# Three weight slots split in place, GLU products and folds on VectorE, convolution taps that alternate between chunks, gate units first, loops written out

## The chip, the cores and the metric

The kernel runs on one core of one Trainium2 chip. Its time is the device time of one launch in microseconds (us). A core has a matrix engine (TensorE, PE in the profile), a vector engine (VectorE, DVE), an activation engine (ScalarE, ACT), a general one (GpSimd, POOL), and a queue that issues transfers (SyncE, SP). Each works through its own program in order; they meet at semaphores only.

## The reference, cut to what matters

Two transformer blocks run over 1024 positions of width 1024, the second also over 256 context positions in its first layer, all in fp32.

```
h = x + swa(rms(x));  h = h + relu(rms(h) @ w_up)**2 @ w_down;  x = rms(h)     # first block
# second block, even layer (for x and for ctx)
a_val, a_glu, a_gate, b_val, b_gate = split(pre(x) @ w_in)                      # five times 512
u   = a_val * sigmoid(a_glu)
u   = silu(layernorm(dwconv31(u) + conv_b))
y_a = (u @ pw + pw_b) * silu(a_gate)
y_b = fourier(b_val) @ fw * silu(b_gate)        # DFT over positions and over groups of 128 channels
x   = x + gate * (concat(y_a, y_b) @ w_out)
# odd layer: cb*dwconv3(cc*cx)*silu(cg) beside RoPE window attention with context keys, then w_out
# out = rms(x)
```

## The kernel before, in words

Activations lie with channels on the 128 partitions and positions along the free axis, in tiles of 512 (TILES1: two tiles; TILES2: these and one of 256 for the context). Every fp32 matmul is made of three (mm3, L188): both operands are cut into a high half of type fp32r and a low half, the rest; high times high, high times low and low times high are summed in PSUM.

The weights are 153 units of 128 x 1024 fp32 (512 KB) in the order in which they are used, counted by stages: qkv 10, wo 8, mlp 64, ein 20 (the even layer's input projection, from E0), dft 6, fw 1, pw 2, eout 8, oin 26 (from O0), oout 8. A unit is loaded by SP (load_unit, L135) into one of two slots wst, its high half is cast by ScalarE (split_hi, L152), and its low half is subtracted by GpSimd (split_lo, L158), into slots wH and wL. In a few places GpSimd makes both halves (split_unit, L141). The copy into a slot waits until TensorE has begun the unit after the one that used it (units_begun), and the load until the low half made from the raw slot is done (weights_split). linear_unit (L194) then runs 48 matmuls for two tiles, or 72 for three, and ScalarE or VectorE drains the banks. The units of a stage are a hardware loop (Fori) over pairs, on each engine.

The program is a sequence of blocks, each ended by a barrier of all engines. The first unit of a stage is split in the block before, the second after the barrier, beside the norm, whose diagonal scalings (norm_sq, L398) and squares (L250, L255) run on VectorE and ScalarE.

In the block of the even input projection (from L1174) the units come as four pairs a_glu, a_val, then four of b_val, then eight gate units. ScalarE drains them into sig and val, bt, or a gate buffer that is stored to memory. GpSimd multiplies sig and val into conv_in; VectorE then runs the 31 taps of the depthwise convolution of chunk c, one after the other (L1294 the first, L1298 the rest; each waits for the one before), 4 x 31 in all, each 128x1295. GpSimd also folds each b_val unit into sums and differences (bf) for the Fourier part, and makes its low half bL after ScalarE's copies to bH:

```
                        pool.tensor_tensor(bf[:, 0:512], bt[:, 0:512], bt[:, 512:1024], ALU.subtract).then_inc(fold_step, 1)
                        pool.wait_ge(fold_step, 2 * g + 1)
                        pool.tensor_tensor(bt[:, 0:512], bt[:, 0:512], bt[:, 512:1024], ALU.add).then_inc(fold_step, 1)
```

The next block (from L1353) has on TensorE: sums of the convolved tiles for the layer norm (L1364), the channel DFT, the DFT over positions with four dft units and three halves out of two more, then the mixing with fw and pw. VectorE meanwhile scales by the reciprocal root (L1506, L1510), and ScalarE applies silu (L1478) and copies high halves (L1480, L1487). In this block GpSimd splits all units alone (stream of split_unit).

Of the kernel before, what the change touches and what calls it, by code (L numbers as in the profile page):

```python
# [24 lines left out]
ALU = mybir.AluOpType  # L25
# [5 lines left out]
P = 128  # L31
# [3 lines left out]
CTX = 256  # L35
# [50 lines left out]
def build(nc, t):  # L86
# [13 lines left out]
    with es:  # L100
# [32 lines left out]
        W_FREE = 2  # L133

        def load_unit(sp, base, i, s):  # L135
            u, slot = base + 2 * i + s, (base + s) % 2
            sp.wait_ge(weights_split, u + 1)
            sp.dma_start(wst[:, slot, :], t["wstream"][bass.ds(u, 1)].rearrange("a p f -> p (a f)"))\
                .then_inc(stage_loaded[slot], 16)

        def split_unit(pool, base, i, s):  # L141
            u, slot = base + 2 * i + s, (base + s) % 2
            pool.wait_ge(stage_loaded[slot], ((base + s) // 2 + 1 + i) * 16)
            pool.wait_ge(units_begun, u + 1)

            pool.tensor_tensor(wH[:, slot, :], wst[:, slot, :], ones[:, 0:1].to_broadcast([P, KC * P]), ALU.mult)\
                .then_inc(weights_hi, 1)
            pool.wait_ge(weights_hi, u + 1)
            pool.tensor_tensor(wL[:, slot, :], wst[:, slot, :], wH[:, slot, :].bitcast(F32), ALU.subtract)\
                .then_inc(weights_split, 1)  # L150

        def split_hi(act, base, i, s):  # L152
            u, slot = base + 2 * i + s, (base + s) % 2
            act.wait_ge(stage_loaded[slot], ((base + s) // 2 + 1 + i) * 16)
            act.wait_ge(units_begun, u + 1)
            act.copy(wH[:, slot, :], wst[:, slot, :]).then_inc(weights_hi, 1)  # L156

        def split_lo(pool, base, i, s):  # L158
            u, slot = base + 2 * i + s, (base + s) % 2
            pool.wait_ge(weights_hi, u + 1)  # L160
            pool.tensor_tensor(wL[:, slot, :], wst[:, slot, :], wH[:, slot, :].bitcast(F32), ALU.subtract)\  # L161
                .then_inc(weights_split, 1)

        def stream(eng, one, lo, hi):

            if (hi - lo) // 2 > 1:
# [1885 lines left out]
```

## Time and profile before

| | |
|---|---|
| timed runs | 2345.18, 2348.38, 2345.18 us; median 2345.18 |
| profiled execution | 2351.11 us, its span 2349.1 us |
| TensorE busy | 2171.5 us (92%), 10132 matmuls; granted clock 0.95 in the mean |
| VectorE busy | 1264.1 us (54%) |
| ScalarE busy | 728.0 us (31%) |
| GpSimd busy | 700.5 us (30%) |
| moved by DMA | 157.16 MB, 67 GB/s in the mean |

Busy times are sums over the span. An engine's share says how full it is, not whether the end of a block waits for it. A row of the timeline is: start, duration, engine, line, operation, output <- inputs, count, and in brackets how long the engine stood before it and what released it.

### The profile page before, as it was taken

The numbers are of one execution on the slowest core, as the hardware profiler recorded it, in microseconds if no ns is written. First come the engines' busy times: TensorE is split into PE (matmuls) and PEld (weight loads), VectorE is DVE, ScalarE is ACT, GpSimd is POOL, SyncE is SP. The second block draws the span as 40 slices with busy tenths as digits, with TensorE's granted clock in tenths as the row PEclk, the third lists the DMA queues.
The fourth block names the chain that finished last, engine by engine and source line by source line (L and its number), as shares of the span: only waits on it lengthen the run. The fifth ranks groups of instructions, "written<-read, shape, count | busy, mean of one in ns | idle before, by whom it ended". The sixth has DMA issues, their size and how long they took to land. (4 is left out here: it accounts for less than half of the span.)

```text
span 2349.1 us, 29236 instructions
## 1 busy us (share of the span) xinstructions
PE 2171.5 (92%) x10132; PEld 1766.1 (75%) x10132; DVE 1264.1 (54%) x1972; ACT 728.0 (31%) x1358; POOL 700.5 (30%) x359
## 2 busy tenths in 40 slices
PE   4999989999999999999889889979989999979896
PEld 3876668788888888888578778668867788766675
DVE  6137852672371371473669999785252122378724
ACT  4236542421221220222442122432152211156522
POOL 4223322322222222222244762142132222234422
PEclk9987889899999999999899989989999999979998
DMA  4100021231231231231201012124121211100031
GB/s 137 67 27 1 1 89 46 81 127 52 72 134 45 76 129 45 89 116 49 113 27 36 29 66 82 56 75 177 36 111 45 81 45 53 45 5 14 10 116 72
DMA packets 42690, 157.16 MB, mean 67 GB/s; under 512 B 4224, under 2 KB 8960, under 8 KB 41344
## 3 DMA queue, kind: packets, MB, share of 16 engines
q1 hardware_dynamic: 40176, 146.49, 17.9%
q10 hardware_dynamic: 2448, 9.84, 1.1%
q8 instruction: 36, 0.59, 0.1%
q14 instruction: 30, 0.25, 0.0%
HBM read 136.39 MB, written 19.92 MB: 67 GB/s over the span
## 5 line engine op out<-in xcount | busy, mean ns | idle before, releaser
L161 POOL TENSOR_TENSOR wL<-wst,wH 128x1024 fp32r<-128x1024 f32 x139 | 360.3, 2592 | 1139.8 <-ACT wH L156 1139.5
L190 PE MATMUL banks<-u2H,wH 128*128 128x512 f32 x736 | 295.7, 402 | 29.4 <-POOL wL L161 18.6
L191 PE MATMUL banks<-u2L,wH 128*128 128x512 f32 x736 | 291.5, 396 | 0.0
L192 PE MATMUL banks<-u2H,wL 128*128 128x512 f32 x736 | 291.1, 396 | 0.0
L190 PE MATMUL banks<-uH,wH 128*128 128x512 f32 x672 | 262.7, 391 | 2.0 <-DVE uL L387 1.5
L191 PE MATMUL banks<-uL,wH 128*128 128x512 f32 x672 | 262.2, 390 | 0.0
L192 PE MATMUL banks<-uH,wL 128*128 128x512 f32 x672 | 262.2, 390 | 0.0
L1298 DVE SCALAR_TENSOR_TENSOR conv_out<-conv_in,par,conv_out x120 | 242.1, 2018 | 21.6 <-DVE conv_out L1298 20.9
L190 PE MATMUL banks<-aH,wH 128*128 128x512 f32 x640 | 249.9, 390 | 2.2 <-PEq L213 2.2
L191 PE MATMUL banks<-aL,wH 128*128 128x512 f32 x640 | 249.5, 390 | 0.0
L192 PE MATMUL banks<-aH,wL 128*128 128x512 f32 x640 | 249.5, 390 | 0.0
L156 ACT CAST wH<-wst 128x1024 fp32r<-128x1024 f32 x139 | 145.3, 1045 | 332.7 <-PE banks L190 326.7
L190 PEld LDWEIGHTS banks<-u2H,wH 128*128 128x128 f32 x736 | 141.4, 192 | 66.3 <-issue 32.3
L1072 DVE TENSOR_TENSOR h<-banks,h 128x512 f32 x64 | 43.9, 690 | 232.3 <-PE banks L192 232.3
L191 PEld LDWEIGHTS banks<-u2L,wH 128*128 128x128 f32 x736 | 141.4, 192 | 29.6 <-issue 1.2
L192 PEld LDWEIGHTS banks<-u2H,wL 128*128 128x128 f32 x736 | 141.0, 192 | 30.2
L1060 DVE SCALAR_TENSOR_TENSOR mod_junk<-mod_w,cvec 128x1024 bf16<-128x1024 f32 x96 | 146.8, 1529 | 14.3 <-DMA mod_w<-in_mod_w 2.8
L190 PEld LDWEIGHTS banks<-uH,wH 128*128 128x128 f32 x672 | 126.6, 188 | 31.5 <-issue 5.1
L192 PEld LDWEIGHTS banks<-uH,wL 128*128 128x128 f32 x672 | 126.6, 188 | 26.6
L191 PEld LDWEIGHTS banks<-uL,wH 128*128 128x128 f32 x672 | 126.7, 189 | 26.2
L190 PEld LDWEIGHTS banks<-aH,wH 128*128 128x128 f32 x640 | 120.5, 188 | 27.6 <-PEq L213 2.6
L191 PEld LDWEIGHTS banks<-aL,wH 128*128 128x128 f32 x640 | 120.5, 188 | 25.1
(279 smaller groups left out, 4012.0 us busy)
## 6 DMA issues: line engine op xcount, KB each, us to landing
wst<-in_wstream SPq DMA_DIRECT2D x153, 512.0 KB, 3.3
mod_w<-in_mod_w SPq DMA_DIRECT2D x48, 512.0 KB, 6.0
x_scratch<-h SPq DMA_DIRECT2D x2, 4096.0 KB, 11.8
gt<-gates_scratch SPq DMA_DIRECT2D x8, 640.0 KB, 4.0
h<-in_x SPq DMA_DIRECT2D x4, 1024.0 KB, 10.7
h<-in_x SPq DMA_DIRECT2D x1, 4096.0 KB, 12.1
h<-x_scratch SPq DMA_DIRECT2D x1, 4096.0 KB, 12.2
xo<-x_scratch SPq DMA_DIRECT2D x1, 4096.0 KB, 12.2
```

The source lines that it names most:

```text
L156: act.copy(wH[:, slot, :], wst[:, slot, :]).then_inc(weights_hi, 1)
L161: pool.tensor_tensor(wL[:, slot, :], wst[:, slot, :], wH[:, slot, :].bitcast(F32), ALU.subtract)\
L190: first = pe.matmul(out, aH, bH, start=start, stop=False)
L191: pe.matmul(out, aH, bL, start=False, stop=False)
L192: return first, pe.matmul(out, aL, bH, start=False, stop=stop)
L1060: dve.scalar_tensor_tensor(mod_junk[:], mod_w[:, m, :], 1.0, cvec[:, v, :], ALU.mult, ALU.mult, accum_out=modv[:, bass.ds(12 * q + 3 * i + ...
L1072: dve.tensor_tensor(dst, bank(4 + s * 2 + ti), dst, ALU.add).then_inc(down_drained, 1)
L1298: dve.scalar_tensor_tensor(dst, src, w, dst, ALU.mult, ALU.add).then_inc(conv_step, 1)
```

## The change

There are three slots, raw, whose low half is written over the raw weights (wL is the same memory), and wH beside them. A load waits for units_begun of the unit two before, and a cast waits for its load alone. ScalarE makes all high halves and GpSimd all low ones (lows). Two units of the next stage are split before a barrier. The loops are written out. In the even projection VectorE makes the products, the folds and the low halves of b; taps alternate over the chunks whose input is there, seven per unit; the gate units come before those of b_val.

```diff
-        wst = sb("wst", [2, KC * P], A_WST)
-        wH = sb("wH", [2, KC * P], A_WHL, F32R)
-        wL = sb("wL", [2, KC * P], A_WHL + 8 * KB, F32R)
-
-
-        stage_loaded = [sem("stage_loaded0"), sem("stage_loaded1")]
+        R = 3
+        raw = sb("raw", [R, KC * P], A_WST)
+        wL = sb("wL", [R, KC * P], A_WST, F32R)
+        wH = sb("wH", [R, KC * P], A_WST + R * 4 * KB, F32R)
...
+        def load_unit(sp, u):
+            if u >= R:
+                sp.wait_ge(units_begun, u - R + 2)
+            sp.dma_start(raw[:, u % R, :], t["wstream"][u]).then_inc(raw_loaded[u % R], 16)
 
         def loads(sp, first, last):
 
-            lo = W0[first] + 3 if W0[first] else 0
-            hi = min(W0[last] + dict(STAGES)[last] + 3, UNITS)
-            stream(sp, load_unit, lo, hi)
-
-        def splits(pool, first, last, done=1):
-
-            lo = W0[first] + done
-            hi = min(W0[last] + dict(STAGES)[last] + 1, UNITS)
-            stream(pool, split_lo, lo, hi)
+            lo = W0[first] + R - 1 if W0[first] else 2
+            for u in range(lo, min(W0[last] + dict(STAGES)[last] + R - 1, UNITS)):
+                load_unit(sp, u)
+
+        def split_hi(act, u):
+            if u < UNITS:
+                act.wait_ge(raw_loaded[u % R], (u // R + 1) * 16)
+                act.copy(wH[:, u % R, :], raw[:, u % R, :]).then_inc(weights_hi, 1)
+
+        def split_lo(eng, u):
+            if u < UNITS:
+                eng.wait_ge(weights_hi, u + 1)
+                eng.tensor_tensor(wL[:, u % R, :], raw[:, u % R, :], wH[:, u % R, :].bitcast(F32), ALU.subtract)\
+                    .then_inc(weights_split, 1)
+
+        def lows(pool, lo, hi):
+            for u in range(lo, hi):
+                split_lo(pool, u)
...
-            pe.wait_ge(weights_split, u + 1 + W_FREE)
+        def linear_unit(pe, u, j0, K, tiles, rhs, bank_of, done, drained, ready=None, off=0):
+
+            pe.wait_ge(weights_split, u + 1)
...
+                    if part == 1:
+                        load_unit(sp, 0)
+                        load_unit(sp, 1)
...
-                split_unit(pool, W0["qkv"], 0, 0)
-                split_unit(pool, W0["qkv"] + 1, 0, 0)
+                split_lo(pool, 0)
+                split_lo(pool, 1)
                 norm1.pool(pool)
-                splits(pool, "qkv", "qkv", 2)
+                lows(pool, 2, W0["wo"] + 2)
...
-                norm1.act(act)
+                norm1.act(act, lambda: (split_hi(act, 0), split_hi(act, 1)))
...
-                with act.Fori(0, 4) as i:
+                for i in range(0, 4):
                     for s in range(2):
                         hi(i, s, lambda ti: aH[:, bass.ds(2 * i + s, 1), TN * ti:TN * ti + TN].rearrange("p a n -> p (a n)"))
-                        split_hi(act, W0["qkv"] + 2, i, s)
+                        split_hi(act, 2 * i + s + 2)
                 hi(4, 0, lambda ti: kH[:, TN * ti:TN * ti + TN])
-                split_hi(act, W0["qkv"] + 10, 0, 0)
+                split_hi(act, 10)
                 hi(4, 1, lambda ti: vT[:, TN * ti:TN * ti + TN])
+                split_hi(act, 11)
...
+                for v in range(4):
+                    i, s = divmod(v, 2)
+                    act.wait_ge(b_lo, v + 1)
+                    for ti, (c0, n) in enumerate(TILES2):
+                        drain(i + 8, s, ti, bt[:, c0:c0 + n], ACT.Copy)
+                    split_hi(act, E0 + 18 + v)
+                    act.wait_ge(folded, v + 1)
+                    act.copy(bH[:, v, 0:SEQ], bf[:]).then_inc(b_hi, 1)
+                    act.copy(bH[:, v, SEQ:TOK], bt[:, SEQ:TOK]).then_inc(b_hi, 1)
...
-                pool.memset(conv_in[:], 0.0).then_inc(ci_zero, 1)
-                pool.wait_ge(ci_zero, 1)
-                with pool.Fori(0, HALF) as i:
-                    for s in range(2):
-                        split_lo(pool, E0 + 2, i, s)
-                    pool.wait_ge(ein_drained, (2 * i + 2) * T3 + E_FREE)
...
+                for at in (0, MAIN0 + SEQ, CTX0 + CTX):
+                    pool.memset(conv_in[:, :, at:at + PAD], 0.0).then_inc(consts_set, 1)
+                lows(pool, E0 + 2, W0["dft"] + 2)
...
+                def product(c):
+                    dve.wait_ge(ein_drained, (2 * c + 2) * T3 + E_FREE)
+                    dve.tensor_tensor(conv_in[:, c, MAIN0:MAIN0 + SEQ], sig[:, 0:SEQ], val[:, 0:SEQ], ALU.mult)
+                    dve.tensor_tensor(conv_in[:, c, CTX0:CTX0 + CTX], sig[:, SEQ:TOK], val[:, SEQ:TOK], ALU.mult)\
+                        .then_inc(ci_ready, 1)
+
+                def fold(g):
+                    dve.wait_ge(ein_drained, (g + 17) * T3 + E_FREE)
+                    dve.tensor_tensor(bf[:, 0:512], bt[:, 0:512], bt[:, 512:1024], ALU.subtract).then_inc(fold_step, 1)
+                    dve.wait_ge(fold_step, 2 * g + 1)
+                    dve.tensor_tensor(bt[:, 0:512], bt[:, 0:512], bt[:, 512:1024], ALU.add).then_inc(fold_step, 1)
+                    dve.wait_ge(fold_step, 2 * g + 2)
+                    dve.tensor_tensor(bf[:, 512:768], bt[:, 0:256], bt[:, 256:512], ALU.subtract)
+                    dve.tensor_tensor(bf[:, 768:1024], bt[:, 0:256], bt[:, 256:512], ALU.add).then_inc(folded, 1)
+
+                def fold_low(g):
+                    dve.wait_ge(b_hi, 2 * g + 2)
+                    dve.tensor_tensor(bL[:, g, 0:SEQ], bf[:], bH[:, g, 0:SEQ].bitcast(F32), ALU.subtract)
+                    dve.tensor_tensor(bL[:, g, SEQ:TOK], bt[:, SEQ:TOK], bH[:, g, SEQ:TOK].bitcast(F32), ALU.subtract)\
+                        .then_inc(b_lo, 1)
+
+                steps, tapped, latest = [0] * HALF, [0], [-1] * HALF
+
+                def taps(n, chunks):
+                    for _ in range(n):
+                        open_ = [c for c in range(chunks) if steps[c] < TAPS]
+                        if not open_:
+                            return
+                        c = min(open_, key=lambda c: latest[c])
+                        tap = steps[c]
+                        src = conv_in[:, c, tap:tap + CONV_OUT]
+                        dst = conv_out[:, c, :]
+                        w = par[:, PC["conv_w"] + c * TAPS + tap:PC["conv_w"] + c * TAPS + tap + 1]
                         if tap == 0:
-                            dve.tensor_scalar(dst, src, w, par[:, bass.ds(c + PC["conv_b"], 1)], ALU.mult, ALU.add)\
-                                .then_inc(conv_step, 1)
+                            dve.wait_ge(ci_ready, c + 2)
+                            dve.tensor_scalar(dst, src, w, pcol("conv_b", c), ALU.mult, ALU.add).then_inc(conv_step, 1)
                         else:
-                            dve.wait_ge(conv_step, c * TAPS + tap)
+                            dve.wait_ge(conv_step, latest[c] + 1)
                             dve.scalar_tensor_tensor(dst, src, w, dst, ALU.mult, ALU.add).then_inc(conv_step, 1)
+                        steps[c], latest[c] = tap + 1, tapped[0]
+                        tapped[0] += 1
+
+                for v in range(20):
+                    if v < 16:
+                        if v == 1:
+                            dve.wait_ge(consts_set, 4 + 3)
+                        if v < 8 and v % 2:
+                            product(v // 2)
+                        taps(7, min((v + 1) // 2, HALF))
+                    else:
+                        fold(v - 16)
+                        taps(4 if v < 18 else HALF * TAPS, HALF)
+                        fold_low(v - 16)
...
-                        loads(sp, "dft", "dft")
+                        for u in range(W0["dft"] + 2, W0["pw"] + 2):
+                            load_unit(sp, u)
+                    if i == 6:
+                        load_unit(sp, W0["eout"])
+                    if i == 7:
+                        load_unit(sp, W0["eout"] + 1)
...
-                stream(pool, split_unit, W0["dft"] + 1, W0["pw"] + 3)
+                lows(pool, W0["dft"] + 2, W0["eout"] + 2)
...
+                split_hi(act, W0["dft"] + 2)
...
+                    if j == 5:
+                        split_hi(act, W0["dft"] + 3)
+                split_hi(act, W0["dft"] + 4)
+                split_hi(act, W0["dft"] + 5)
...
+                    if j in (3, 7, 15):
+                        split_hi(act, W0["fw"] + (3, 7, 15).index(j))
...
-    units += [ein[12:16], ein[8:12], ein[16:20]]
+    units += [ein[8:12], ein[16:20], ein[12:16]]
```

The first place is ScalarE at the end of the block that projects q, k and v. Before, with kH and vT the last two units drained and the second branch the barrier:

```order
L156 CAST wH<-wst 128x1024 [waits units_begun]
L539 REGISTER_ALU
L539 COMPARE_AND_BRANCH
L538 CAST kH<-banks 128x512 [waits qkv_done] x2
L156 CAST wH<-wst 128x1024 [waits units_begun,stage_loaded0]
L538 COPY vT<-banks 128x512 [waits qkv_done] x2
L498 UNCONDITIONAL_BRANCH
L818 UNCONDITIONAL_BRANCH [waits barrier_Pool_Activation_PE_DVE_SP_release]
```

After:

```order
L149 CAST wH<-raw 128x1024 [waits raw_loaded0]
L515 CAST kH<-banks 128x512 [waits qkv_done] x2
L149 CAST wH<-raw 128x1024 [waits raw_loaded1]
L515 COPY vT<-banks 128x512 [waits qkv_done] x2
L149 CAST wH<-raw 128x1024 [waits raw_loaded2]
L473 UNCONDITIONAL_BRANCH
L795 UNCONDITIONAL_BRANCH [waits barrier_Pool_Activation_PE_DVE_SP_release]
```

One cast (raw_loaded2, unit 11, the second of the next stage) has moved in ahead of the barrier, behind the copy to vT, which was the last work of the block. The odd projection ends in the same way.

The second place is VectorE in the even projection. Before, the whole of it is this loop over a chunk's taps (the branch ahead of it enters it):

```order
L1287 UNCONDITIONAL_BRANCH
L1287 ISA
L1294 ISA [waits ci_ready]
L1294 ISA
L1294 REGISTER_ALU
L1294 TENSOR_SCALAR conv_out<-conv_in,par 128x1295
L1297 REGISTER_ALU
L1298 ISA [waits conv_step]
L1298 SCALAR_TENSOR_TENSOR conv_out<-conv_in,par,conv_out 128x1295
```

After, its last rows, for the last two units of b_val, which are units 18 and 19 of the stage:

```order
L1229 TENSOR_TENSOR bf<-bt 128x512 [waits ein_drained]
L1231 TENSOR_TENSOR bt<-bt 128x512 [waits fold_step]
L1233 TENSOR_TENSOR bf<-bt 128x256 [waits fold_step]
L1234 TENSOR_TENSOR bf<-bt 128x256
L1259 SCALAR_TENSOR_TENSOR conv_out<-conv_in,par,conv_out 128x1295 [waits conv_step] x11
L1238 TENSOR_TENSOR bL<-bf,bH 128x1024 [waits b_hi]
L1239 TENSOR_TENSOR bL<-bt,bH 128x256
L1238 TENSOR_TENSOR bL<-bf,bH 128x1024 [waits b_hi]
L1239 TENSOR_TENSOR bL<-bt,bH 128x256
L1140 UNCONDITIONAL_BRANCH
L1481 UNCONDITIONAL_BRANCH [waits barrier_Pool_Activation_PE_DVE_SP_release]
```

The last eleven taps now stand between the fold of unit 18 and its low halves, and the low halves of unit 19 are the last work before the barrier; its fold (four rows like the first four) stands between them.

The third place is ScalarE in the block of the Fourier part. Before, ahead of and among the silu jobs (zH is the channel DFT, ln_rs the root, sH the high half of a silu):

```order
L1467 CAST zH<-banks 128x512 [waits ln_z_done] x2
L1472 ACT_TABLE_LOAD
L1472 ACTIVATE ln_rs<-banks,eps 128x512 [waits ln_sq_used] x2
L1472 ACTIVATE ln_rs<-banks,eps 128x256 [waits ln_sq_used]
L1478 ACT_TABLE_LOAD
L1478 ACTIVATE conv_out<-conv_out,par 128x512 [waits ln_v]
L1480 CAST sH<-conv_out 128x512 [waits ln_silu]
```

After, up to the first silu job:

```order
L1447 CAST zH<-banks 128x512 [waits ln_z_done] x2
L149 CAST wH<-raw 128x1024 [waits raw_loaded2]
L1453 ACT_TABLE_LOAD
L1453 ACTIVATE ln_rs<-banks,eps 128x512 [waits ln_sq_used] x2
L1453 ACTIVATE ln_rs<-banks,eps 128x256 [waits ln_sq_used]
L1459 ACT_TABLE_LOAD
L1459 ACTIVATE conv_out<-conv_out,par 128x512 [waits ln_v]
L1461 CAST sH<-conv_out 128x512 [waits ln_silu]
```

and behind the last silu jobs:

```order
L1459 ACTIVATE conv_out<-conv_out,par 128x256 [waits ln_v]
L1461 CAST sH<-conv_out 128x256 [waits ln_silu]
L149 CAST wH<-raw 128x1024 [waits raw_loaded1]
L149 CAST wH<-raw 128x1024 [waits raw_loaded2]
L1472 ACTIVATE fH<-banks 128x512 [waits dft_done] x4
L149 CAST wH<-raw 128x1024 [waits raw_loaded0]
L1472 ACTIVATE fH<-banks 128x256 [waits dft_done]
```

Four casts of weights have come in, ahead of the root, behind the sixth job (not shown), and two between the last silu and the first fH; a fifth follows the fourth fH. They are work that GpSimd did.

## Rows read from the trace of the kernel before

**Rows 1.** A window of the MLP: us, busy times, PEclk, DMA share, GB/s.

```profile
840.00:900.00 60.00, 60.00 (x267) 49.67 (x266) 34.92 (x43) 12.33 (x17) 15.80 (x6) 1.00 0.30 105
```

**Rows 2.** The page: the span, TensorE's busy time, and one VectorE group.

```profile
span 2349.1 us, 29236 instructions
PE 2171.5 (92%) x10132; PEld 1766.1 (75%) x10132; DVE 1264.1 (54%) x1972; ACT 728.0 (31%) x1358; POOL 700.5 (30%) x359
L1072 DVE TENSOR_TENSOR h<-banks,h 128x512 f32 x64 | 43.9, 690 | 232.3 <-PE banks L192 232.3
```

**Rows 3.** The waits of TensorE: us in total, times, longest.

```profile
PE banks L190 <- POOL wL L161: 18.6, 4, 6.5
```

**Rows 4.** Windows of the even projection, and of its last five units.

```profile
1205.00:1475.60 270.60, 255.81 (x1297) 219.02 (x1296) 241.94 (x122) 58.03 (x87) 129.22 (x50) 0.96 0.15 53
1406.66:1475.60 68.94, 68.86 (x360) 59.19 (x358) 62.82 (x36) 14.52 (x22) 14.51 (x5) 1.00 0.23 86
```

**Rows 5.** The timeline of ScalarE behind unit 1 of the even projection.

```profile
1205.41 1.04 ACT L156 CAST wH<-wst 128x1024 fp32r<-128x1024 f32 x1
```

**Rows 6.** The timeline of VectorE where one chunk's taps end.

```profile
1418.08 1.57 DVE L1298 SCALAR_TENSOR_TENSOR conv_out<-conv_in,par,conv_out  x1 [0.18 <-DVE conv_out L1298]
1419.56 0.95 DVE L1294 TENSOR_SCALAR conv_out<-conv_in,par  x1
...
1424.19 3.44 DVE L1298 SCALAR_TENSOR_TENSOR conv_out<-conv_in,par,conv_out  x1 [0.18 <-DVE conv_out L1298]
```

**Rows 7.** The timeline of GpSimd in the even projection.

```profile
1408.89 2.40 POOL L161 TENSOR_TENSOR wL<-wst,wH 128x1024 fp32r<-128x1024 f32 x1 [13.55 <-ACT wH L156]
1422.59 3.67 POOL L161 TENSOR_TENSOR wL<-wst,wH 128x1024 fp32r<-128x1024 f32 x1 [11.30 <-ACT wH L156]
```

**Rows 8.** The timeline at the end of the even projection.

```profile
1479.08 1.57 DVE L1298 SCALAR_TENSOR_TENSOR conv_out<-conv_in,par,conv_out  x1 [0.18 <-DVE conv_out L1298]
...
1480.97 2.04 PE L1364 MATMUL banks<-conv_out,ones 128*128 128x512 f32 x2 [5.45 <-PEq L1174]
```

**Rows 9.** The timeline of the Fourier part and the mixing.

```profile
1514.58 1.90 POOL L146 TENSOR_TENSOR wH<-wst,ones 128x1024 fp32r<-128x1024 f32 x1 [47.54 <-PE banks L190]
...
1518.58 6.74 DVE L1510 SCALAR_TENSOR_TENSOR conv_out<-conv_out,par,ln_rs 128x512 f32<-128x512 f32 x4
...
1558.08 0.58 PE L190 MATMUL banks<-wH,zH 128*128 128x256 f32 x1 [10.46 <-DVE fL L1518]
...
1568.03 0.47 PE L190 MATMUL banks<-fH,wH 128*128 128x512 f32 x1 [1.96 <-DVE fL L1518]
...
1608.29 0.49 PE L190 MATMUL banks<-yH,wH 128*128 128x512 f32 x1 [2.26 <-PEq L213]
```

**Rows 10.** The timeline of VectorE at the start.

```profile
18.38 5.60 DVE L398 TENSOR_SCALAR norm_sq<-ident,rms_cols 128x128 f32<-128x128 f32 x4
23.90 8.20 DVE L255 TENSOR_TENSOR x_squares_acc<-x_squares_acc,x_squares_sq 128x512 f32<-128x512 f32 x8
```

**Rows 11.** The timeline at the end of the projection of q, k, v.

```profile
148.07 0.59 ACT L538 COPY vT<-banks 128x512 f32<-128x512 f32 x1 [4.85 <-PE banks L192]
...
148.96 0.29 PE L190 MATMUL banks<-kH,aH 64*128 64x128 f32 x1 [0.93 <-PEq L498]
```

**Rows 12.** The timeline of the norm ahead of the MLP.

```profile
422.21 3.23 PE L355 MATMUL banks<-inv_d,wo_squares_acc 128*128 128x1 f32 x16 [2.79 <-PEq L912]
...
424.28 3.01 DVE L398 TENSOR_SCALAR norm_sq<-ident,rms_cols 128x128 f32<-128x128 f32 x4
...
427.35 3.78 PE L360 MATMUL banks<-norm_sq,ones 128*128 128x512 f32 x4 [1.91 <-DVE norm_sq L398]
427.41 0.87 DVE L398 TENSOR_SCALAR norm_sq<-ident,rms_cols 128x128 f32<-128x128 f32 x4
```

**Rows 13.** The timeline at the end of the odd projection.

```profile
2042.90 0.62 ACT L1742 CAST ycH<-cw 128x512 fp32r<-128x512 f32 x1 [0.32 <-DVE cw L1820]
...
2044.87 0.59 PE L190 MATMUL banks<-k2H,qH 64*128 64x256 f32 x2 [3.44 <-PEq L1624]
```

More of the change, by code:

```diff
@@ L562, in lo @@
                             .then_inc(qkv_drained, 1)
-                with dve.Fori(0, 4) as i:
+                for i in range(0, 4):
                     for s in range(2):
@@ L943, in _ @@
                 dve.wait_ge(x_again, 16)
-                with dve.Fori(0, 4) as i:
+                for i in range(0, 4):
                     for s in range(2):
@@ L1001, in hidden @@
                 def hidden(q):
-                    with act.Fori(0, 4) as i:
+                    for i in range(0, 4):
                         for s in range(2):
@@ L1042, in hidden @@
                 def hidden(q):
-                    with dve.Fori(0, 4) as i:
+                    for i in range(0, 4):
                         for s in range(2):
@@ L1065, in down @@
                 def down(q, squares=None):
-                    with dve.Fori(0, 4) as i:
+                    for i in range(0, 4):
                         for s in range(2):
@@ L1106, in _ @@
                 down(0)
-                with pe.Fori(1, QUARTERS) as q:
+                for q in range(1, QUARTERS):
                     up(q, 0)
@@ L1286, in _ @@
                 norm4.dve(dve)
[L1287 to L1292 removed]
+                dve.sem_inc(ci_ready, 1)
+                dve.sem_inc(b_lo, 1)
@@ L1408, in _ @@
                     u = D0 + 4 + min(half, 1)
-                    slot = begin(u) if half < 2 else u % 2
+                    slot = begin(u) if half < 2 else u % R
                     if half == 0:
@@ L1580, in _ @@
                 dve.wait_ge(x_back, 32)
-                with dve.Fori(0, 4) as i:
+                for i in range(0, 4):
                     for s in range(2):
@@ L1715, in _ @@
                 act.sem_inc(S["ag_stored"], 16)
-                with act.Fori(0, 2) as i:
+                for i in range(0, 2):
                     for s in range(2):
@@ L1743, in branch @@
                             .then_inc(S["yc_hi"], 1)
-                    if not last:
-                        split_hi(act, O0 + 15, 2 * i, 0)
-                with act.Fori(0, 3) as i:
-                    branch(i, False)
-                branch(3, True)
+                    split_hi(act, O0 + 15 + 4 * i)
+                for i in range(4):
+                    branch(i)
             @block.vector
@@ L1780, in _ @@
                     rot_lo(0, ti, k2H[:, TN * ti:TN * ti + TN], k2L[:, TN * ti:TN * ti + TN])
-                with dve.Fori(0, 2) as i:
+                for i in range(0, 2):
                     for s in range(2):
@@ L1795, in _ @@
                 dve.wait_ge(S["prod_zero"], 2)
-                with dve.Fori(0, 4) as i:
+                for i in range(0, 4):
                     for ti in range(2):
@@ L1896, in _ @@
                 dve.wait_ge(x_back, 32 + 16)
-                with dve.Fori(0, 4) as i:
+                for i in range(0, 4):
                     for s in range(2):
```

264 lines of the change are left out of this document (82 added, 182 removed).

## The prediction

> **What bounds the kernel now.** I read the windows view first. In the linear stages TensorE is busy the whole 60.00 us of a window at a granted clock of 1.00, with 267 matmuls in it, about 0.225 us apart [rows 1]. There a weight unit of 48 matmuls takes 10.9 us. The page's span of 2349.1 us can only shrink where TensorE stands still, 177.6 us in all (2349.1 - 2171.5 us) [rows 2]. So I read TensorE's waits next. 18.6 us of them, in 4 waits with a longest of 6.5 us, are put down to GpSimd's low halves [rows 3]; the unit is cut late where GpSimd folds in between. Then come the windows of the even projection: from the end of unit 1 at 1205 to the end of unit 19 at 1475.6 TensorE idles 14.8 us (270.60 - 255.81) and the clock is 0.96; in the last five units it is 1.00 and a unit takes 13.8 us (68.94 / 5) [rows 4]. Eighteen units at 13.8 us are 248.2 us, so stalls and the low clock behind them cost 22.4 us. But that is not what the stage's end waits for: the last tap of the convolution ends at 1480.65, and only 0.3 us later, at 1480.97, TensorE starts the next block [rows 8]. VectorE is the second bound.
>
> **The change part by part**, in the time of the profiled execution.
>
> *Slots, loads, unrolling: 0 in the linear stages.* A unit must be loaded, cut (1.04 us of ScalarE [rows 5]) and subtracted within 10.9 us, before and after; the old order does it, since TensorE never waits there [rows 1], and the new one asks for the same work with a slot more. The window is full across loop ends too, so the gain of unrolling is 0 by it. The Trainium skill, page "Runtime: NRT & Kernel Launch", section "Instruction fetch mechanics", says that a taken branch can force a fetch stall; by that rule the sum would come out lower.
>
> *Even projection: -7.6.* TensorE loses its three stalls: unit n now ends at 1205.0 + 13.78 (n - 1), unit 16 at 1411.7, unit 18 at 1439.3, unit 19 at 1453.0. What then ends last is VectorE. A tap of the same chunk takes 1.57 us and waits 0.18 for the one before, together 1.75; behind another chunk it need not wait, and the one such row starts 1.48 us after its predecessor (1419.56 less 1418.08) [rows 6]. A tap that meets a GpSimd subtract takes 3.44 us for 1.57, and the subtract 3.67 us for 2.40 [rows 6, 7]: they take turns, and one low half per unit costs VectorE about 1.9 us. So seven alternated taps and one meeting are 12.3 us, under the 13.8 us of a unit; the first two units, with one open chunk, are 14.2 us, and the four products add 1.5 us each (an estimate: 1280 columns to a tap's 1295 [rows 6]). VectorE is through with unit 15's taps near 1401 and idles until unit 16 ends. Units 16 and 17: fold 2.5 + 2.4 (one meeting), four taps 6, low halves 1.5, together 12.4 us, in time. The tail begins at unit 18, 1439.7: fold 4.8, to 1444.5; eleven taps, four of them serial, 17.4; low halves 1.6, to 1463.5. Only now may ScalarE drain unit 19 (its buffer was in use): 1.4. Fold 4.8, the two copies 1.6, low halves 1.5, barrier 0.4: the next block starts at 1473.4, against 1480.97. Of the 22.4 us only 7.6 arrive, and TensorE stands about 20 us at the end instead. The Trainium skill, page "GPSIMD Engine Reference", section "Key points", says that GpSimd contends with VectorE instructions that have two SBUF inputs; the trace agrees, with 3.44 against 1.57 us. Bounds: without meetings in the tail -12.4; with all its taps serial (+1.9) and another meeting (+1.9) -3.8.
>
> *Transform and mixing, 1480.97 to 1608.29: -5.* Before, GpSimd made both halves (1.90 and some 2.4 us [rows 7, 9]) of six units while VectorE normalised, and four scalings took 6.74 us, which are 2.8 us at the 0.69 us that an operation of this size takes elsewhere [rows 2]. Now GpSimd makes four low halves there and the high halves sit in ScalarE's queue behind the silu jobs. I add up: the first cut delays ScalarE's root by 1.0; scalings and roots run undisturbed, so ScalarE is through six silu jobs at 1528.8 and cuts the fourth matrix, which is ready at 1532.3; TensorE wants it at 1530.2 and waits 2. All twelve jobs end at 1535.8, the fifth matrix is ready at 1539.3, TensorE waits 1.5, and its three halves of 5.8 us (48 matmuls of 256 columns, some 0.12 us each, an estimate) end at 1556.7 where before the last began at 1558.08, after the 10.46 us wait. The mixing starts near 1558.7 instead of 1568.03: -9.3. It gives back some: ScalarE waits for the unit of the pointwise weights, whose load can't start before the mixing does, so the first copies are 3 us late and TensorE ends 1.9 us later relative to its start. For two or three new short waits and the clock behind them I add 2.4, since each old stall in the projection cost 2.6 us of clock besides itself ((22.4 - 14.8) / 3) but shorter ones cost less. Bounds: -9 with no clock loss, +2 if the two waits and the late copies are double.
>
> *Start: -1.9.* Four diagonal scalings took 5.60 us beside GpSimd's two casts and two subtracts, and the second tile's squares ended at 32.1 [rows 10]. Now ScalarE casts before those squares (+2.1 on its side), the scalings take 0.87, as four of them do where GpSimd is idle [rows 12], and two subtracts remain: squares end near 30.2. Bounds -4 and +1 (weights now load before the second half of the input).
>
> *Ends of blocks: +8.0.* Every block ends in a barrier. Units n and n + 1 of the next stage are now cut before it, where the second was cut behind it. After the projection of q, k, v the last copy ends at 148.66 and TensorE starts at 148.96 [rows 11]; now 1.04 + 0.1 + 2.40 + 0.3 follow: 152.4, +3.4. Before the window attention likewise from 2043.52: 2047.4 for 2044.87, +2.5 [rows 13]. Before the MLP the barrier moves from 422.2 to 424.8, but there the 3.01 us of diagonals, in which GpSimd was in the way, become 0.87, so that the spread starts right after the 3.23 us of sums, at 428.0 for 427.35: +0.7 [rows 12]. The even and the odd projection begin with the same norm: +0.7 each. Bounds: 6 and 11.
>
> Sum: 0 - 7.6 - 5.0 - 1.9 + 8.0 = -6.5, hence 2344.6 us for the profiled execution's 2351.1. The three timed runs have a median of 2345.18, 5.9 us under it; taken off the median the sum gives **2338.7 us**.
>
> **Rivals.** (a) *The transform stage doesn't gain* (0 to +3 for -5): the matrices come late from ScalarE because its queue is in order. For it: eight cuts now stand between other jobs. Against it: VectorE is freed of some 15 us of meetings. About 2345, within 0.2%. (b) *Slower:* the alternated taps don't start earlier than 1.75 us. Then seven taps and a meeting are 14.2 us, more than a unit's 13.8, VectorE falls behind, the first fold starts near 1424, and the tail ends near 1489: +8 for -7.6, so 2354. It decides as soon as taps plus meeting exceed 13.8 us. Against it stands the one row of 1.48 us. (c) *More gain:* the tail has no meetings (-4.8) and the transform stage gives 9: 2330. (d) *Unrolled code starves an engine* and each linear unit gets a gap. The window of 267 matmuls would show it as idle time; 0.1 us for each of 139 units would be +14, 2352. Against it: the even transform's code is straight already, and its matmuls follow each other without gaps.
>
> **How the numbers follow.** Likeliest 2338.7, own range 2332 to 2345, chance 0.55; (a) 0.22; (b) 0.08; (c) 0.10; (d) 0.05. 0.2% is 4.7 us, about what a measurement of this kernel can tell from no change: faster is below 2340.5, slower above 2349.9. Of the likeliest case some 0.40 lies below 2340.5; with (c) and a little else faster is 0.52; slower 0.14; same 0.34. The range 2329 to 2349 leaves out (b), (d) and the far side of (c).
>
> **What would show it.** In the profile after: no wait on a GpSimd low half from 1205 to 1453 on TensorE; taps 1.48 us apart; a TensorE gap of about 20 us at the end of the even projection and a block start 7.6 us earlier relative to unit 1's end; the 10.46 us wait gone and two waits of 1 to 3 us on the new low halves before it; gaps of 4.4 and 6 us instead of 0.93 and 3.44 ahead of the two attentions; windows of 60.00 us busy in the MLP. Wrong would be: gaps inside linear units, or a tail that ends elsewhere than on VectorE.

## The result and the profile after

The changed kernel takes 2415.9 us in the median of four runs (2413.70 to 2417.95), where the kernel before took 2345.38 beside it: a ratio of 1.0293, 95% interval 1.0278 to 1.0308. It is 70.5 us slower. The forecast was 2338.7, with a range of 2329 to 2349. The profiled execution has a span of 2414.5 us, 65.4 more than before.

The page of the changed kernel: the span, the busy times, and the groups of the low halves and of the taps.

```profile
span 2414.5 us, 25481 instructions
PE 2162.0 (90%) x10132; PEld 1759.5 (73%) x10132; DVE 1215.8 (50%) x2004; ACT 733.1 (30%) x1366; POOL 687.1 (28%) x315
...
L154 POOL TENSOR_TENSOR wL<-raw,wH 128x1024 fp32r<-128x1024 f32 x153 | 490.5, 3207 | 1374.9 <-ACT wH L149 1374.9
...
L1259 DVE SCALAR_TENSOR_TENSOR conv_out<-conv_in,par,conv_out 128x1295 f32<-128x1295 f32 x120 | 181.4, 1579 | 0.6
```

TensorE has as many matmuls as before and is busy 9.5 us less [rows 2], so all of the loss is standing still: 252.5 us (2414.5 - 2162.0) where it was 177.6. Two rows say more than they seem to. A low half takes 3207 ns in the mean, though the same operation takes 2.40 us undisturbed [rows 7]: 153 times 0.8 is over 120 us of waiting inside the operation. (In the serial run below the mean is 2612 ns, so some 30 us of it are there without the stall too.) And the taps have 0.6 us of idle time ahead of them in all 120.

TensorE's waits after the change, answering to [rows 3]: us in total, times, longest.

```profile
PE banks L163 <- POOL wL L154: 81.3, 4, 71.5
...
PE banks L1342 <- PEq L1140: 18.2, 1, 18.2
PE banks L163 <- DVE win_pTL L739: 16.1, 20, 3.3
PE banks L163 <- DVE stat L728: 15.6, 4, 9.3
PE banks L163 <- PEq L185: 7.4, 3, 3.4
PE banks L163 <- PEq L1608: 5.8, 1, 5.8
```

One wait of 71.5 us is as large as the whole loss. The timeline of the changed kernel's GpSimd in the even projection shows where it comes from, and those of ScalarE, VectorE and TensorE around it what it is:

```profile
1242.31 11.50 POOL L154 TENSOR_TENSOR wL<-raw,wH 128x1024 fp32r<-128x1024 f32 x1 [11.26 <-ACT wH L149]
1256.09 2.50 POOL L154 TENSOR_TENSOR wL<-raw,wH 128x1024 fp32r<-128x1024 f32 x1 [2.28 <-ACT wH L149]
1269.87 11.47 POOL L154 TENSOR_TENSOR wL<-raw,wH 128x1024 fp32r<-128x1024 f32 x1 [11.28 <-ACT wH L149]
1283.65 2.50 POOL L154 TENSOR_TENSOR wL<-raw,wH 128x1024 fp32r<-128x1024 f32 x1 [2.31 <-ACT wH L149]
1297.95 83.31 POOL L154 TENSOR_TENSOR wL<-raw,wH 128x1024 fp32r<-128x1024 f32 x1 [11.81 <-ACT wH L149]
```

```profile
1310.59 1.04 ACT L149 CAST wH<-raw 128x1024 fp32r<-128x1024 f32 x1 [0.41 <-ACT val L1158]
```

```profile
1286.47 0.96 DVE L1256 TENSOR_SCALAR conv_out<-conv_in,par 128x1295 f32<-128x1295 f32 x1
1287.34 91.72 DVE L1259 SCALAR_TENSOR_TENSOR conv_out<-conv_in,par,conv_out 128x1295 f32<-128x1295 f32 x62
```

```profile
1381.31 0.80 PE L163 MATMUL banks<-u2H,wH 128*128 128x512 f32 x1 [71.55 <-POOL wL L154]
```

The subtract had its input at 1297.95 and nothing else to wait for, yet it ends at 1381.26. The 62 taps end at 1379.06 (1287.34 + 91.72), 2.2 us earlier, and 2.4 us is what a subtract takes by itself: of the 81 us before it got nothing done. The two of 11.5 us end in the same way, 2.3 us behind the end of a run of 14 taps. The next cast (1310.59) was in time, so the load and ScalarE are not it. Windows of the changed kernel: the one of the MLP, and then two behind the wait (columns as in [rows 1]).

```profile
840.00:900.00 60.00, 60.00 (x266) 49.70 (x265) 33.54 (x40) 12.47 (x17) 17.24 (x6) 1.00 0.23 79
```

```profile
1381.30:1386.30 5.00, 4.99 (x12) 3.92 (x13) 0.00 (x0) 0.00 (x0) 2.29 (x1) 0.51 0.40 108
1386.30:1521.70 135.40, 135.36 (x710) 116.62 (x708) 36.50 (x31) 27.21 (x42) 22.45 (x9) 1.00 0.22 65
```

Linear stages are full as before. Behind the wait the granted clock is 0.51 for 5 us, the lower of its two levels, which costs 2.5 more: 74.0 us in all, more than the 65.4 by which the span grew. The rest of the execution is 8.6 us shorter.

### The profile page after: what moved, and what is told of

Its sections match the earlier page's. It is cut to its first block and busy times, and to the rows that moved or that the text cites. A ratio compares the mean times of both kernels' runs of the same rounds, so it can differ in the third digit from the quotient of the medians.

```text
span 2414.5 us, 25481 instructions
## 1 busy us (share of the span) xinstructions
PE 2162.0 (90%) x10132; PEld 1759.5 (73%) x10132; DVE 1215.8 (50%) x2004; ACT 733.1 (30%) x1366; POOL 687.1 (28%) x315
## 5 line engine op out<-in xcount | busy, mean ns | idle before, releaser
L154 POOL TENSOR_TENSOR wL<-raw,wH 128x1024 fp32r<-128x1024 f32 x153 | 490.5, 3207 | 1374.9 <-ACT wH L149 1374.9
L149 ACT CAST wH<-raw 128x1024 fp32r<-128x1024 f32 x153 | 159.5, 1045 | 281.3 <-DMA raw<-in_wstream 276.5
L1259 DVE SCALAR_TENSOR_TENSOR conv_out<-conv_in,par,conv_out 128x1295 f32<-128x1295 f32 x120 | 181.4, 1579 | 0.6
L1039 DVE TENSOR_TENSOR h<-banks,h 128x512 f32<-128x512 f32 x64 | 43.9, 689 | 230.8 <-PE banks L165 230.8
L1027 DVE SCALAR_TENSOR_TENSOR mod_junk<-mod_w,cvec 128x1024 bf16<-128x1024 f32 x96 | 156.6, 1632 | 5.0
L165 PEld LDWEIGHTS banks<-aH,wL 128*128 128x128 f32 x640 | 120.5, 188 | 25.2
```

The costliest lines, as they stand in the source:

```text
L149: act.copy(wH[:, u % R, :], raw[:, u % R, :]).then_inc(weights_hi, 1)
L154: eng.tensor_tensor(wL[:, u % R, :], raw[:, u % R, :], wH[:, u % R, :].bitcast(F32), ALU.subtract)\
L165: return first, pe.matmul(out, aL, bH, start=False, stop=stop)
L1027: dve.scalar_tensor_tensor(mod_junk[:], mod_w[:, m, :], 1.0, cvec[:, v, :], ALU.mult, ALU.mult, accum_out=modv[:, bass.ds(12 * q + 3 * i + ...
L1039: dve.tensor_tensor(dst, bank(4 + s * 2 + ti), dst, ALU.add).then_inc(down_drained, 1)
L1259: dve.scalar_tensor_tensor(dst, src, w, dst, ALU.mult, ALU.add).then_inc(conv_step, 1)
```

## The experiments

Theory A is read from the rows above: a GpSimd operation on SBUF gets nothing done while VectorE's operations follow each other without idle time, and the alternation removes the idle time. Rivals are that GpSimd is slow by itself (B: low half written over its input, code written out) and that a load or cast is late (C).

**VectorE paced, taps as they are.**

```diff
+                        if v >= 8:
+                            dve.wait_ge(ein_drained, (v + 1) * T3 + E_FREE)
                         taps(7, min((v + 1) // 2, HALF))
```

> Edit to the changed kernel: from unit 8 of the even projection on, VectorE waits before each seven taps until that unit has been drained; the same taps in the same order. Theory A (a GpSimd subtract gets nothing while VectorE's taps follow each other without any idle time, so the 63 taps behind the last product, 92 us, lock it out): a run is now 7 taps, 10.4 us, and VectorE idles some 3 us per unit; the subtract ends about 2.3 us after each run, in time for TensorE; the wait of 71.5 us and about 8 us of low clock behind it are gone, 2336 to 2340 us. Theory B (the stall is GpSimd's own: unrolled code, or the low half written over its input): the wait stays, about 2415 us. Theory C (a late load or a late cast): it stays too.

2344.29 us, ratio to the kernel before 0.9981 (0.9967 to 0.9995). GpSimd in the stretch of the long wait, this run:

```profile
1285.10 2.50 POOL L154 TENSOR_TENSOR wL<-raw,wH 128x1024 fp32r<-128x1024 f32 x1 [2.31 <-ACT wH L149]
1299.40 2.39 POOL L154 TENSOR_TENSOR wL<-raw,wH 128x1024 fp32r<-128x1024 f32 x1 [11.81 <-ACT wH L149]
1313.17 2.40 POOL L154 TENSOR_TENSOR wL<-raw,wH 128x1024 fp32r<-128x1024 f32 x1 [11.38 <-ACT wH L149]
```

The long wait is gone with the same GpSimd code, slots and loads, so B and C fall. The subtract doesn't even wait for the end of a run of seven: VectorE's pause 1.5 us before it is enough. The time is some us above the 2336 to 2340 expected, though no wait was left there; by the ratio it is 2340.9.

**Taps chunk by chunk again.**

```diff
-                        c = min(open_, key=lambda c: latest[c])
+                        c = open_[0]
```

> Edit to the changed kernel: the taps go chunk by chunk instead of alternating, seven per unit as before, so that each waits 0.18 us for the one before. No pause between units. Theory A: these 0.18 us are enough to let the subtract in, as in the kernel before; no long wait on TensorE, subtracts of 2.4 to 3.7 us. VectorE needs about 14.2 us per unit of 13.8 and comes late to the folds, 2345 to 2356 us. Theories B and C: about 2415 us or more.

2341.75 us, ratio 0.9972 (0.9957 to 0.9988). A subtract, and the tap that meets it:

```profile
1298.14 3.62 POOL L154 TENSOR_TENSOR wL<-raw,wH 128x1024 fp32r<-128x1024 f32 x1 [11.62 <-ACT wH L149]
```

```profile
1299.54 3.58 DVE L1259 SCALAR_TENSOR_TENSOR conv_out<-conv_in,par,conv_out 128x1295 f32<-128x1295 f32 x1
```

They take turns, as in [rows 6, 7]. The idle time between taps is not 0.18 us but 0.03 to 0.04: written-out serial taps start 1.60 us apart (1296.34, 1297.94, 1299.54 in the trace), so seven and a meeting are 13.2 us and fit into a unit. VectorE isn't late, and my 2345 to 2356 was too high.

**One tap in four serial.**

```diff
-                        c = min(open_, key=lambda c: latest[c])
+                        c = (max if tapped[0] % 4 == 3 else min)(open_, key=lambda c: latest[c])
```

> Edit to the changed kernel: every fourth tap stays in the chunk of the tap before it, the others alternate, so one tap in four waits 0.18 us. Theory A: the subtract gets in at the next such tap, at most about 6 us after it asks, so its time in the profile is 2.4 to 8.5 us; no long wait on TensorE, 2335 to 2342 us. If a gap of 0.18 us lets it in only by chance, some waits of 5 to 30 us remain. Theories B and C: about 2415 us.

2342.53 us, ratio 0.9978 (0.9967 to 0.9989). No subtract in the stage takes over 3.80 us. That is better than expected: it was let in at the first tap boundary after it asked, also at boundaries without idle time. So what counts is not a gap at the boundary itself; hence the two runs after the next.

**The alternation alone, in the kernel before.**

```diff
-                with dve.Fori(0, HALF) as c:
-                    dve.wait_ge(ci_ready, c + 2)
+                at = 0
+                for c0 in (0, 2):
+                    dve.wait_ge(ci_ready, c0 + 3)
                     for tap in range(TAPS):
...
-                            dve.wait_ge(conv_step, c * TAPS + tap)
...
+                        for c in (c0, c0 + 1):
...
+                                dve.wait_ge(conv_step, at - 1)
...
```

> Edit to the kernel before, nothing else of the change: the taps of chunks 0 and 1 alternate, 62 in a row, then those of chunks 2 and 3, written out. Theory A: each run of 62 taps, 92 us, locks GpSimd out, with its low halves, its products and its folds: TensorE stands twice, 60 to 80 us each, about 2480 to 2520 us, slower by over 100. Theory B (in-place halves or unrolled GpSimd code are the cause): no such wait here, 2330 to 2350 us.

2472.35 us in its one run, a little under the 2480 to 2520 expected. TensorE's waits, and GpSimd's first long subtract:

```profile
PE banks L190 <- POOL wL L161: 148.3, 3, 72.2
```

```profile
1247.21 84.41 POOL L161 TENSOR_TENSOR wL<-wst,wH 128x1024 fp32r<-128x1024 f32 x1 [8.35 <-ACT wH L156]
```

Separate slots, looped GpSimd code, the old order of units, and the same stall twice: the second such subtract takes 84.40 us. This edit also writes the taps out, but so is the code of the serial run, which has no stall. So of the whole change the alternation is the cause by itself.

**How rare may the pause be?** One tap in eight, and one in sixteen, stays in its chunk (the same line with 8 and 16).

> Edit to the changed kernel: every eighth tap stays in the chunk of the one before it. In the run with every fourth the subtract was let in at the first tap boundary after it asked, also where that tap followed without idle time, and only up to three taps behind such a gap; in the changed kernel it asked seven taps behind the last gap and was not let in. Theory A1 (a gap protects the next few boundaries, then GpSimd is locked out until the next gap): some subtracts take 2.4 to 4 us, others up to about 13 us, until the next tap in the same chunk; TensorE hardly waits, 2335 to 2345 us. Theory A2 (any such tap in the run undoes the lock-out altogether): none over 4 us.

> Edit to the changed kernel: every sixteenth tap stays in the chunk of the one before it. Theory A1: subtracts of up to about 25 us, ending 2.3 us behind such a tap or the end of a run, and where two meet a unit's time of 13.8 us TensorE waits 5 to 15 us: 2345 to 2370 us. Theory A2: no subtract over 4 us, 2335 to 2342 us. If only the end of a run of taps lets it in, as in the changed kernel, 2415 us.

2343.67 and 2340.87 us in one run each. With eight, one subtract takes 4.23 us and all others under 3.8. Two of these others asked (that is, started) 3.6 and 3.3 us behind a pause of VectorE, with the next over 10 us away (the pauses are at 1334.8, 1348.9 and 1363.0), and didn't wait for it:

```profile
1338.44 3.16 POOL L154 TENSOR_TENSOR wL<-raw,wH 128x1024 fp32r<-128x1024 f32 x1 [10.94 <-ACT wH L149]
1352.22 3.47 POOL L154 TENSOR_TENSOR wL<-raw,wH 128x1024 fp32r<-128x1024 f32 x1 [10.62 <-ACT wH L149]
```

With sixteen, GpSimd in the timeline:

```profile
1325.60 2.71 POOL L154 TENSOR_TENSOR wL<-raw,wH 128x1024 fp32r<-128x1024 f32 x1 [11.38 <-ACT wH L149]
1339.38 10.30 POOL L154 TENSOR_TENSOR wL<-raw,wH 128x1024 fp32r<-128x1024 f32 x1 [11.07 <-ACT wH L149]
1353.16 3.10 POOL L154 TENSOR_TENSOR wL<-raw,wH 128x1024 fp32r<-128x1024 f32 x1 [3.48 <-ACT wH L149]
1366.94 10.69 POOL L154 TENSOR_TENSOR wL<-raw,wH 128x1024 fp32r<-128x1024 f32 x1 [10.69 <-ACT wH L149]
```

The first long one of these ends at 1349.68; a tap with a pause before it starts at 1347.45. I counted, for each subtract that met VectorE at its products and taps, in the changed kernel and the runs with four, eight and sixteen, how many operations VectorE had begun since its last pause when the subtract asked. Up to five: let in at once or at the next boundary, 44 times of 44. Seven or more (7, 7, 8, 8, 9 and three times 11): seven of eight waited until the next pause or the end of the run, and the eighth (11, with sixteen) had asked 0.05 us before a boundary. None asked at six. The alternation in the kernel before fits in: both of its long subtracts asked at seven. So A1 is right in kind; A2 is wrong. Whether it is the number of operations that counts or the time since the pause can't be told from this: the fives asked 7.0 us behind it, the sevens 8.3 and more. TensorE stood for none of it, since a unit leaves 11 us to spare, and so the 2345 to 2370 expected with sixteen was too high.

**Does it take two tensor inputs?**

```diff
-                            dve.scalar_tensor_tensor(dst, src, w, dst, ALU.mult, ALU.add).then_inc(conv_step, 1)
+                            if sum(steps) >= 42:
+                                dve.tensor_scalar(dst, src, w, pcol("conv_b", c), ALU.mult, ALU.add).then_inc(conv_step, 1)
...
```

> Edit to the changed kernel: the taps behind the last product are made by an operation with one tensor input (times a column, plus a column); they don't read what they sum into, so the sum over the taps is left out. They still alternate without idle time. Theory A, narrow (only operations with two tensor inputs lock GpSimd out): subtracts of about 2.4 us there, no long wait of TensorE, about 2340 us. Theory A, wide (any VectorE operations that follow each other without idle time do): the run is 62 x 0.87, some 54 us long, the first subtract in it takes over 40 us and TensorE waits some 30: about 2375 us.

2370.35 us in its one run, near the 2375 expected of the wide theory. GpSimd's first subtract in the stretch, and VectorE's run:

```profile
1300.30 45.26 POOL L154 TENSOR_TENSOR wL<-raw,wH 128x1024 fp32r<-128x1024 f32 x1 [11.81 <-ACT wH L149]
```

```profile
1289.68 53.68 DVE L1260 TENSOR_SCALAR conv_out<-conv_in,par 128x1295 f32<-128x1295 f32 x62
```

TensorE waits 33.5 us. Operations with one tensor input lock GpSimd out as well; these take 0.87 us for 1295 columns, against 1.48 for the taps. The Trainium skill, page "GPSIMD Engine Reference", section "Key points", names two-input instructions and those in a two-port mode; whether these fast ones are of the second sort, no run here shows.

**The low halves on VectorE.**

```diff
-                lows(pool, E0 + 2, W0["dft"] + 2)
...
+                        split_lo(dve, E0 + 2 + v)
                         taps(7, min((v + 1) // 2, HALF))
...
                         fold(v - 16)
+                        split_lo(dve, E0 + 2 + v)
```

> Edit to the changed kernel: in the even projection VectorE makes the low halves of the weights too, one per unit behind its product or fold, and GpSimd none; taps alternate fully. Theory A: nothing is left to be locked out, and waiting for ScalarE's cast once per unit paces VectorE. No wait of TensorE on a low half in the stage; folds without a meeting (2.3 us for 4.3), so the tail is some 16 us for 18: 2335 to 2340 us where the kernel before has 2345. If the low halves overload VectorE (7 taps 10.4, one subtract 1.2, half a product 0.8: 12.4 of 13.8 us), it is above 2350.

2340.80 us, ratio 0.9971 (0.9958 to 0.9984). A low half takes 1.22 us there, half of GpSimd's 2.40, TensorE never waits inside the stage, and the wait at its end is 15.2 us for 18.2.

```profile
1395.50 1.22 DVE L154 TENSOR_TENSOR wL<-raw,wH 128x1024 fp32r<-128x1024 f32 x1 [2.21 <-ACT wH L149]
```

**The cast before the last drain**, on the kernel with one serial tap in four:

```diff
-                hi(4, 1, lambda ti: vT[:, TN * ti:TN * ti + TN])
                 split_hi(act, 11)
+                hi(4, 1, lambda ti: vT[:, TN * ti:TN * ti + TN])
...
```

> Edit to the kernel of the run with every fourth tap: at the end of each stage but the even projection, ScalarE casts the second unit of the next stage before it drains or squares the last unit, not after. Theory (the prediction's term: this cast and its subtract stand between the last drain and the barrier, +3.4 and +2.4 us ahead of the two attentions): these 5.8 us come back; ahead of the three norms the wait of 4.7 to 5.1 us shrinks by about 2.3 each, 7 us. Together 2327 us, against 2340 of its base. Rival (the cast is late anyway because its load is): no more than 2 us.

2327.10 us, ratio 0.9911 (0.9890 to 0.9932): 15.7 us under its base by the ratios and 9.9 by the spans (2338.8 and 2328.9), some 13 expected. Ahead of the first attention:

```profile
145.69 0.29 PE L163 MATMUL banks<-kH,aH 64*128 64x128 f32 x1 [0.93 <-PEq L473]
```

The 0.93 of [rows 11] is back, and ahead of the second attention 3.35. The casts had been late only by their place in ScalarE's queue.

**All of it.** One version has the low halves on VectorE and the earlier casts, with eight taps per unit from unit 3 on and the last cast of the even projection moved too. Another has besides the cast for the second pointwise unit moved behind the sixth copy out of the mixing (the expectation says fifth; the code counts from 0). Out of the two diffs:

```diff
-                        taps(7, min((v + 1) // 2, HALF))
+                        taps(8 if v >= 3 else 7, min((v + 1) // 2, HALF))
...
-                    if j in (3, 7, 15):
-                        split_hi(act, W0["fw"] + (3, 7, 15).index(j))
+                    if j in (3, 7):
+                        split_hi(act, W0["fw"] + (3, 7).index(j))
...
+                    if j == 5:
+                        split_hi(act, W0["fw"] + 2)
```

> Edits to the changed kernel, together: VectorE makes the low halves of the even projection's weights, as in the run before; eight taps per unit instead of seven from unit 3 on, so that none is left for the last two units; each stage's last cast of the next stage's weights before the last drain, in the even projection too. Theory: behind the last unit of the even projection stand only the drain 0.4, the fold 2.2, the two copies 1.5, the low halves 1.6 and the barrier 0.4, some 6 us for 18, and less low clock behind it; the 12.7 us of the ends come with it: 2308 to 2315 us where the kernel before has 2345. If eight taps are too many (8 x 1.48 + 1.2 + 0.8 = 13.9 of 13.8 us while the products last) VectorE comes late to the first fold and TensorE waits there: 2318 to 2325.

> Edit to the kernel of the first run of this call: in the block of the Fourier part the cast of the second pointwise unit, which waits for a load that can't start before the mixing does, moves from ahead of ScalarE's first copy out of the mixing to behind the fifth. Theory (this cast holds up the first copies by 4.7 us and with them VectorE and TensorE): the mixing, 44.0 us where it took 40.3 before the change, is 2 to 3.5 us shorter. Rival (the mixing is longer for the clock, which was low in three stretches of it): no more than 1 us.

2316.79 us, ratio 0.9864 (0.9846 to 0.9881), without the last edit; 2306.03, ratio 0.9816 (0.9800 to 0.9832), with it. The first is 2313.5 by its ratio, within the 2308 to 2315 expected. The end of the even projection is as computed:

```profile
1448.98 1.19 PE L1355 MATMUL banks<-conv_out,ones 128*128 128x512 f32 x1 [5.96 <-PEq L1146]
```

The mixing without and with the last edit, from its first row to the next block's:

```profile
1531.73 0.47 PE L163 MATMUL banks<-fH,wH 128*128 128x512 f32 x1 [1.96 <-DVE fL L1520]
...
1575.45 0.47 PE L163 MATMUL banks<-yH,wH 128*128 128x512 f32 x1 [2.08 <-PEq L185]
```

```profile
1528.80 0.56 PE L163 MATMUL banks<-fH,wH 128*128 128x512 f32 x1 [1.96 <-DVE fL L1522]
...
1568.74 0.47 PE L163 MATMUL banks<-yH,wH 128*128 128x512 f32 x1 [2.07 <-PEq L185]
```

43.7 us become 39.9, so the late cast was worth 3.8, a little over the 2 to 3.5 expected, and its rival, the clock, is out: it is 0.96 in both stretches. The spans differ by 9.2 (2317.3 and 2308.1): 2.9 arise before the mixing and 2.5 behind it, where the programs are the same; that part is no effect of the edit. By the ratio this last version is 43 us faster than the kernel before (0.0184 of 2345.38), by the spans 41.0 (2349.1 - 2308.1).

## Why the prediction was wrong

**The step that failed** is in the even projection: "they take turns, and one low half per unit costs VectorE about 1.9 us". It was read from taps that each waited 0.18 us for the one before [rows 6, 7], and applied to taps from which the same change takes that wait away. The price of the meeting was right wherever VectorE pauses (3.58 and 3.62 us in the serial run); what I missed is that the pause was the condition of taking turns. Without it GpSimd got nothing done in 81 us. Where the text says that VectorE "idles until unit 16 ends", nothing in the program kept the idling in every unit: behind the fourth product no tap waits for anything, so 63 of them run as one. The alternation and the long run are both needed; either undone alone (serial taps, paced taps) removes the stall.

None of the four rivals was this. (b) had the right suspect, VectorE, and the wrong mechanism: the taps did start 1.48 us apart, and it was their being faster that did the harm.

**The rest of the sum** can be judged on the run with one serial tap in four, which has all of the change and no lock-out. Stretches of TensorE's timeline, us:

| stretch | before | change | with 1 in 4 | difference | predicted |
|---|---|---|---|---|---|
| start to the first unit | 38.26 | 34.96 | 35.01 | -3.3 | -1.9 |
| to the first attention | 110.70 | 114.10 | 114.09 | +3.4 | +3.4 |
| to the first unit of the MLP | 282.78 | 276.44 | 276.67 | -6.1 | +0.7 |
| to the even projection | 730.39 | 731.04 | 730.80 | +0.4 | +0.7 |
| to the Fourier block | 318.84 | 383.27 | 309.57 | -9.3 | -7.6 |
| to the output projection | 127.32 | 126.01 | 127.49 | +0.2 | -5.0 |
| to the odd projection | 122.00 | 125.53 | 125.48 | +3.5 | +0.7 |
| to the second attention | 314.58 | 316.63 | 317.42 | +2.8 | +2.5 |
| to the end | 304.23 | 306.52 | 302.30 | -1.9 | 0 |
| sum | 2349.1 | 2414.5 | 2338.8 | -10.3 | -6.5 |

*Even projection.* Its own part came nearly as reckoned, -9.3 for -7.6: stalls gone, the end of the stage on VectorE, TensorE standing 18.5 us there where I had about 20. The lock-out adds 73.7 (383.27 - 309.57), about the 71.55 of the wait and the 2.5 of low clock.

*Ends of blocks.* +3.4 and +2.8 for +3.4 and +2.5 ahead of the two attentions, and the run with the earlier casts gave them back: for these two, mechanism and size were right. Ahead of the odd projection the size was not, as told below.

*Transform and mixing.* The mixing starts 83.4 us into the block for 87.1 before (1549.57 less 1466.14), -3.6 where I had -9.3, and takes 3.8 longer (44.1 for 40.3), for which I had 1.9; I had 2.4 more for waits and clock. The 5.7 us missing at the start of the mixing are there step by step: TensorE starts the fourth matrix 52.6 us into the block for my 51.3; it is 7.4 us at it for 5.5, at a granted clock of 0.77; it waits 2.52 for the fifth for 1.5 (4.14 in the changed kernel, 4.13 in the first version of all of it); and the last halves take 19.0 us for 17.4, at a clock of 0.91. So rival (a) holds here, no gain: the matrices came later and the clock behind the two waits cost more than the 2.4 set aside for both.

*Loops.* 60.00 of 60.00 us busy before and after: the linear stages got nothing from being written out, and (d) is out. The Trainium skill, page "Runtime: NRT & Kernel Launch", section "Instruction fetch mechanics", says that a taken branch forces a fetch stall when its target isn't among the pages at hand; in this window there was no stall to remove.

*Not foreseen:* -6.1 in the stretch with the first attention, whose code hardly changes. The granted clock there is 0.84 before and 0.87 to 0.88 after, and TensorE is busy 253.5 us before and 243.1 to 244.8 after for the same 1217 matmuls, which is enough for it; why the clock differs was not tested. And +3.5 ahead of the odd projection for +0.7: the run with the earlier casts has 120.9 us there for 125.5, so this too was the cast's place in the queue. The -3.3 at the start lies within the bounds that I gave for it; the -1.9 in the last stretch was not looked into.

So the sum without the lock-out, -10.3 by the spans and -5 by the ratio of that run, lies near the forecast of -6.5, but in part by luck: the unforeseen gain of 6.1 stands against the 5.2 that the transform and mixing fell short.

## What to carry to other kernels

When VectorE's dependent operations are interleaved so that none waits, ask who else works in SBUF: a GpSimd operation that TensorE needs can be held until VectorE next pauses, here for 81 us. Keep a pause at least every few operations (one serial operation in four or eight cost nothing here), give VectorE a semaphore per unit, or give it GpSimd's operation, which it did in half the time. And a price read from a trace holds under the conditions of that trace: ask whether the change removes them.

## What the runs showed of the hardware

- A 128x1024 subtract of GpSimd took 2.40 us alone, up to 3.8 us against VectorE operations with 0.03 us between them, and 83.31, 84.41, 84.40 and 45.26 us against runs of VectorE operations without idle time; each of these ended 2.2 us behind the run. VectorE lost nothing in them: its taps stayed at 1.48 us.
- The lock-out sets in only some operations behind a pause: none was seen up to five (7.0 us), and in the same four runs seven of eight subtracts were locked out at seven or more. Why it isn't there at once, and whether operations or time count, stays open.
- A tap of VectorE that needs the one before it waited 0.18 us in the loop of the kernel before [rows 6], which has register operations between its taps, and 0.03 to 0.04 us in written-out code. That the register operations make the difference was not tested.
- TensorE's granted clock was 0.51 for 5 us behind a wait of 71.5 us, and 0.50 for about as long (5.3 us) behind a wait of 18.5 us, in the run with one serial tap in four.
